# Late index products spread unevenly over the units of the first output projection, and four moves of single steps elsewhere

## The reference: two layers of a decoder trunk

```python
# layer 0
h = rms_norm(x, g);  z = h @ w_in                    # q, k, v, index q/k/w, u, v_b
logits = einsum('bqhe,bse->bqhs', qi, ki)            # 8 index heads of width 32
score  = einsum('bqh,bqhs->bqs', wi, relu(logits))   # causal
idx    = top_k(score, 256)                           # the keys that a query attends to
x = x + concat(a_out, b_out) @ w_out                 # sparse attention, spatial gating
x = x + square(relu(rms_norm(x) @ w1)) @ w2          # MLP, hidden 4096
# layer 1
y = conv31(glu(rms_norm(x) @ w_pw1)) + b;  x = x + silu(rms_norm(y, g_conv)) @ w_pw2
x = x + square(relu(rms_norm(x) @ w1)) @ w2
```

## Time and profile before

| | us |
|---|---|
| median of 3 runs | 2062.2 |
| the profiled execution | 2062.01 |
| its span, first to last instruction | 2060.3 |
| PE busy | 2028.5 |
| DVE busy | 1554.9 |
| ACT busy | 1040.8 |
| POOL busy | 863.9 |

### The profile page before, as it was taken

How to read it: one execution, slowest core, us unless ns; L and a number is a source line. 1 busy time by engine, 2 the same in 40 slices (tenths; PEclk the granted TensorE clock), 3 DMA queues, 4 the chain that set the end, 5 groups by cost and what they waited for, 6 DMA issues and landing times.

```text
span 2060.3 us, 28332 instructions
## 1 busy us (share of the span) xinstructions
PE 2028.5 (98%) x9594; PEld 1696.0 (82%) x9594; DVE 1554.9 (75%) x2238; ACT 1040.8 (51%) x1575; POOL 863.9 (42%) x572
## 2 busy tenths in 40 slices
PE   7999899999999999999999999999999999999999
PEld 7788788888889878888888888888878888888887
DVE  6698758988854377977888745889863577979877
ACT  6644666756446547453323256445365346463562
POOL 5864674654560110045646456858664700000000
PEclk9999999999999999999999999999999999999999
DMA  5221022423221245323232232323352463434433
GB/s 215 93 72 62 32 83 84 142 93 101 73 72 44 73 137 202 131 75 110 92 103 93 92 102 93 102 93 134 128 187 85 161 215 113 163 133 143 154 123 123
DMA packets 83043, 233.11 MB, mean 113 GB/s; under 512 B 7648, under 2 KB 8032, under 8 KB 81376
## 3 DMA queue, kind: packets, MB, share of 16 engines
q1 hardware_dynamic: 79312, 225.09, 32.5%
q10 hardware_dynamic: 3600, 6.32, 0.8%
HBM read 214.60 MB, written 16.78 MB: 112 GB/s over the span
## 4 chain that ended last, share of the span: by engine, by line
PE 83%; DVE 7%; issue 3%; POOL 3%; ACT 2%; DMA 1%; DVEq 0%; ACTq 0%; POOLq 0%; SPq 0%
PE psum L1077 16%; PE psum L1079 16%; PE psum L1078 16%; PE psum L1407 9%; PE psum L1408 9%; PE psum L1409 9%; PE psum L1252 3%; PE psum L1102 2%; DVE small L2614 2%; DVE score L2612 2%; PE psum L1228 1%; POOL w_buf L1464 1%; PE psum L1229 1%; DMA raw<-weights 1%; DVE psum L2862 1%
## 5 line engine op out<-in xcount | busy, mean ns | idle before, releaser
L1464 POOL TENSOR_TENSOR w_buf<-raw,w_buf 128x1024 fp32r<-128x1024 f32 x218 | 531.8, 2441 | 529.5 <-ACT w_buf L1834 508.4
L1834 ACT ACTIVATE w_buf<-raw 128x1024 fp32r<-128x1024 f32 x204 | 214.8, 1054 | 204.0 <-PE psum L1079 137.8
L1407 PE MATMUL psum<-hid_buf,w_buf 128*128 128x512 f32 x776 | 302.0, 389 | 1.4 <-issue 1.4
L1408 PE MATMUL psum<-hid_buf,w_buf 128*128 128x512 f32 x776 | 301.9, 389 | 0.0
L1409 PE MATMUL psum<-hid_buf,w_buf 128*128 128x512 f32 x776 | 301.9, 389 | 0.0
L1077 PE MATMUL psum<-hid_buf,w_buf 128*128 128x512 f32 x768 | 300.0, 391 | 1.0 <-POOL hid_buf L1632 1.0
L1078 PE MATMUL psum<-hid_buf,w_buf 128*128 128x512 f32 x768 | 299.1, 389 | 0.0
L1079 PE MATMUL psum<-hid_buf,w_buf 128*128 128x512 f32 x768 | 299.0, 389 | 0.0
L1078 PE MATMUL psum<-h_buf,w_buf 128*128 128x512 f32 x768 | 298.8, 389 | 0.0
L1079 PE MATMUL psum<-h_buf,w_buf 128*128 128x512 f32 x768 | 298.8, 389 | 0.0
L1077 PE MATMUL psum<-h_buf,w_buf 128*128 128x512 f32 x768 | 298.8, 389 | 0.0
(11 more groups left out here) (379 smaller groups left out, 3648.5 us busy)
## 6 DMA issues: line engine op xcount, KB each, us to landing
raw<-weights SPq DMA_DIRECT2D x298, 512.0 KB, 3.5
w_more<-weights SPq DMA_DIRECT2D x66, 512.0 KB, 4.1
xt<-x_t SPq DMA_DIRECT2D x2, 2048.0 KB, 8.8
x_early<-xt SPq DMA_DIRECT2D x2, 2048.0 KB, 10.2
h_first<-x_early SPq DMA_DIRECT2D x2, 2048.0 KB, 8.5
out_t<-xt SPq DMA_DIRECT2D x16, 256.0 KB, 2.0
x_in<-x_t SPq DMA_DIRECT2D x12, 256.0 KB, 6.4
m_kept<-m_ring ACTq DMA_DIRECT2D x12, 256.0 KB, 2.0
```

Source lines behind the costliest of these rows:

```text
L1407: nc.tensor.matmul(acc, hi, b_split(v, 0, j), start=start, stop=False, skip_group_check=True)
L1408: nc.tensor.matmul(acc, hi, b_split(v, 1, j), start=False, stop=False, skip_group_check=True)
L1464: nc.gpsimd.tensor_tensor(dst_lo, src, dst_hi.bitcast(F32), ALU.subtract).then_inc(done, 1)
L1834: nc.scalar.activation(w_buf[:, 0, :, slot * P:(slot + 1) * P], raw[:, slot % 2], ACT.Copy).then_inc(hi_up, 1)
```

## The change: counts for the products, room for the groups, and three reordered lists

- `late_logits`: units 0 to 7 get 2, 2, 2, 5, 5, 5, 5, 6 products instead of 4 each. `logits_behind` places them within a unit: behind steps 1 and 3 of a half unit; behind steps 0, 2, 3, 5, 7 with five; 0, 1, 3, 4, 5, 7 with six.
- `late_groups_at`: the unit before the last unit up of each 16 (u = 6, 22, 38) counts half. By the formula unit 7 has one group instead of two, 8 two instead of one, 17 two instead of one, 18 one instead of two, 21 two instead of one, 22 none instead of two, 23 two instead of one, 31 three instead of two, 38 one instead of two.
- `pre`: the mean stands before step 6 of block (1, 1, 0), six matmuls earlier.
- `split_first`: the weights of pair 0 are split behind unit 5, the first half of activations 1 behind unit 6; before, the other way round.
- `pair_splits`: in session 0 the copies of products 4 and 5 stand in step 4, behind the two splits of activations 2; before, in steps 5 and 6.

```diff
-    at = [sum(cost[:n + 1]) * len(free) / sum(cost) for n in range(len(cost))]
-    return [tiles for tiles, when in zip(LATE_GROUPS, at) if free.index(u) < when <= free.index(u) + 1
-            or (u == free[-1] and when > len(free))]
+    room = [0.5 if at % 16 == 6 else 1.0 for at in free]
+    before = sum(room[:free.index(u)])
+    at = [sum(cost[:n + 1]) * sum(room) / sum(cost) for n in range(len(cost))]
+    return [tiles for tiles, when in zip(LATE_GROUPS, at) if before < when <= before + room[free.index(u)]
+            or (u == free[-1] and when > sum(room))]
...
+LATE_COUNTS = (2, 2, 2, 5, 5, 5, 5, 6)
+
 def late_logits(m):
-    return range(LOGITS[LATE] + 4 * m, LOGITS[LATE] + 4 * m + 4)
+    first = LOGITS[LATE] + sum(LATE_COUNTS[:m])
+    return range(first, first + LATE_COUNTS[m])
+
+def logits_behind(logits, k, steps):
+    return [n for at, n in enumerate(logits) if (at + 1) * steps // len(logits) - 1 == k]
...
-                    if k % 2 and logits:
-                        index_logits(logits[k // 2])
+                    for n in logits_behind(logits, k, KT):
+                        index_logits(n)
...
-                    if logits:
-                        index_logits(logits[k])
+                    for n in logits_behind(logits, k, 4):
+                        index_logits(n)
...
                             for k in range(4 * kh, 4 * kh + 4):
+                                if (i, kh, r, k) == (1, 1, 0, 6):
+                                    mean_of("conv1", sum_lo)
...
-                            if (i, kh, r) == (1, 1, 0):
-                                mean_of("conv1", sum_lo)
...
                 if i and r == 1:
+                    split_weights(0)
+                if i and r == 2:
                     split_activations(1, 0)
-                if i and r == 2:
-                    split_weights(0)
...
-                    if g > first and copied(g - 1):
+                    if g > first and copied(g - 1) and not (session == 0 and g in (5, 6)):
                         copy_product(g - 1)
...
                     if session == 0 and g == 4:
                         split_activations(2, 0)
                         split_activations(2, 1)
+                        copy_product(4)
+                        copy_product(5)
```

## The result

The changed kernel takes 2065.9 us, the median of 22 runs (2064.0 to 2069.5); the kernel before took 2062.2 on the same chip (22 runs, 2061.5 to 2064.5). The ratio is 1.0016 [1.001, 1.0022]: slower by 3.7 us, which is within the 0.2% that counts as no change, but on the other side of it than the forecast (2061.2), and outside its range (2059.1 to 2063.0). The profiled execution took 2065.06 us with a span of 2063.3, 3.0 more than before.

The account below looks back on a forecast made before the run. PE was taken as the bound, busy 2028.5 of 2060.3 us, so only its stalls could change. The terms -0.65 - 0.1 - 1.4 + 1.2 = -0.95 took 2062.0 to 2061.1, median 2061.2 us, range 2059.1 to 2063.0.

Parts of the forecast that it names:

- the hidden tiles: Hidden tile 7 at 469.47 and 557.04: the first stall of 1.04 goes, the second grows by 0.95; net -0.1.
- the session: Session 0: stalls of 0.72 ahead of it and 1.68 at product 8 go, 0.97 returns at product 10; net -1.4.
- the mean of ff0 0: Stall at 340.10, behind the late products of wout 0: grows by 0.4, to 0.9 idle.
- Product 10: In session 0: waits for the copy of product 6, 0.7 idle, so 0.85 + 0.1 come back.
- the second hidden tile: Hidden tile 7 at 557.04: POOL's weights for unit 42 delay tile 39, stall grows by 0.95 to about 1.2 idle.
- the last rival: All four moves work as aimed, the mean of conv1 costs nothing: -6.3, 2055.9 us; chance 0.03.
- Late products: Part on wout 0: product stalls fall from 2.36 to 1.3, gain 1.05; mean of ff0 0 +0.4; net -0.65.
- the hand schedule: Units 0 to 3 of wout 0 worked forward by durations, engines in list order: two late products in unit 3, 0.3 and 0.8.
- The mean of conv1: At 1503.28: PE asks 1.36 us earlier, the sums come no earlier, 2.4 idle; +1.2, bounds 0 and +2.7.
- the wait at 1520: A PE wait of 0.2 behind the mean of conv1, which the shift of 1.2 to 1.4 may swallow.
- The spread only moves its waits: Rival on wout 0: unit 3 stalls for all that units 1 and 2 did, gain of 1.05 gone, 2062.2; chance 0.15.
- The other side: Rival: conv1's early mean delays weights three or four blocks on, 1.2 becomes 2.7, sum +0.5, 2062.7; chance 0.12.

Follow-up runs that it names:

- the first: The changed kernel with four late products in each unit as before, the other moves kept: 2063.2 us, ratio 1.0004.
- the seventh experiment: The changed kernel without the new product counts and without the early mean of conv1, leaving the top-k groups and session 0 moves: 2060.7 us, ratio 0.9989.
- the fourth: The changed kernel with the squares of wout 0 written by ACT to PSUM, so their sum has one SBUF input: 2061.2 us, ratio 0.9995.
- the fifth: The changed kernel with squares in PSUM and the mean of conv1 back behind its block: 2059.9 us, ratio 0.9988.
- the second experiment: The kernel before with the new counts of late products alone: 2065.0 us, ratio 1.0016.
- the third experiment: The changed kernel with the sum of squares of row 1 moved behind the residual of row 2 on DVE: 2061.9 us, ratio 0.9995.

## Why the prediction was wrong

**The bound and the method were right.** The work of PE didn't change, and stall by stall the traces add up: -1.04 and +0.9 at the hidden tiles and -1.4 in the session, as forecast, and +0.2 at the mean of ff0 0 (0.4 forecast). Product 10 is 0.78 idle (0.7 forecast), the second hidden tile 1.15 (1.2), no stall stands ahead of the session or at product 8. The third product of unit 3, for which 0.3 + 0.1 were forecast, isn't late. One share was reckoned wrong: 4.1 us is half of the 8.4 of all touched stalls and two thirds only of the 6.3 of the last rival.

**The step that failed** is in "Late products": "DVE does for it a residual and a sum of squares (0.68 each)". By the hand schedule "the residual of row 2 on DVE (299.9), which stands behind the low input of row 1", and the sum of squares between them was put in at its price without POOL. POOL's next weights were in that schedule as well: the relu behind ACT's split of unit 6 ends there at 299.2, so the split at about 298.6, and POOL has the low part of unit 6 from then to 301.0. The sum of squares, behind the low input (298.1) and a sum (0.6), begins at about 298.7, inside it. I had the rule for exactly this in the same part, from the Trainium skill ("SBUF — State Buffer", section "SBUF: two separate sides"), and applied it to the low input alone. By that rule the sum of squares, which also has two inputs in SBUF, isn't done until POOL is: the trace agrees (2.68 us, 0.55 past POOL's end, and 0.67 from PSUM). The residual was short beside POOL at all times; it has one input in PSUM.

In the rows of before only the low input is long, but these rows end at 331.9. Behind them the same trace has another such hold, the split of the sums, which took 2.77 us (DVE and POOL of the kernel before):

```profile
337.28 2.77 DVE L2431 TENSOR_TENSOR sum_lo<-sq_sum,sum_hi 128x512 fp32r<-128x512 f32 x1
336.94 2.55 POOL L1464 TENSOR_TENSOR w_buf<-raw,w_buf 128x1024 fp32r<-128x1024 f32 x1 [7.27 <-ACT w_buf L1834]
```

It too has two inputs in SBUF, and the stall at 340.10 waits for it, in the changed kernel as before; the +0.4 there was worked out from DVE's list alone. In the ten traces, from 286 to 345 us, 78 low inputs, sums of squares and splits of sums begin more than 0.15 us ahead of the end of POOL's weights. Every one ends 0.54 to 0.56 behind that end. What hid the hold of the sum of squares: in the kernel before, each of the six up to 325 us begins after one of POOL's weights has ended and ends before the next begins (the second from 300.13 to 300.81, POOL at work until 299.13 and from 301.82), so 0.68 was their price without POOL. The new spread makes both engines earlier, but not by the same: less the 1.08 of the start-up, this sum comes at 298.9 instead of 300.1, and POOL's next weights at 298.7 instead of 301.8.

**The term mis-sized.** -1.05 was forecast and +2.62 measured. Of the 3.7 between them, 2.2 is the longer stall (3.01 instead of 0.8) and about 1.5 the clock. The prediction said that a stall costs its idle time + 0.27. That holds up to some size. In the ten traces (before, after and eight experiments) the clock fell behind both stalls of 3.01, behind one of five at the early mean of conv1 (2.07 to 2.33 idle) and behind two of ten at the one near 216 us (1.65 to 1.69); behind none of 0.2 to 1.44 did it fall. The bounds of this part, -2.4 and +0.6, left out a hold of the sum of squares; the upper one should have had the wait for one more of POOL's instructions.

**The mean of conv1.** At full clock it cost 0.7 (alone in the kernel before), 0.8 (between the first and the seventh experiment) and 1.2 (between the fourth and the fifth), against +1.2 forecast. In the trace of the changed kernel PE loses 1.08 there, and 0.3 come back by 1525 us: the wait at 1520, of which the prediction said that it may be swallowed, is gone. What the prediction lacked is the price in clock: among the four kernels of the experiments that have the early mean, 23 of 44 runs are below 1.000; among the three experiments without it (and without the stall of 3.01), 6 of 29, and of the kernel before 15 of 61. The four are uneven: 7, 6, 3 and 7 of 11. The changed kernel (13 of 22 at 0.998) fits this, against 3 of 11 at 0.998 in the second experiment, which has the stall of 3.01 without the early mean. The trace of the third experiment shows the place once; in the four other traces with the early mean the clock held there. So that the early mean costs clock is likely and not shown, as a run leaves one trace.

**The rivals.** None of them was this. "The spread only moves its waits" had the place and the direction, but as a zero and not as a loss. The other side was sought at conv1, where it isn't.

**Open.** The trace doesn't say what decides whether the clock falls after an idle time of about 2 us. Executions of one kernel differ in it.

## What to carry to other kernels

When a schedule by hand uses a hold of one engine by another, apply it to every instruction of that kind in the stretch, not only to the one that the old trace shows lengthened: moving work changes which of them meets the other engine. Two remedies worked here: put the instruction that others wait for ahead of the one that can be held, or let one of its inputs come from PSUM. And a stall of PE of 2 us or more can cost more than its length, also where it is only asked for earlier: a wait brought forward by 1.4 us cost 0.7 to 1.2 at once, and half of the executions with it lost about 2 us of clock somewhere, against a quarter of those without.

## What was not expected of the hardware

- The same sum of 128x512 fp32 on DVE took 0.68 us alone, 1.60 and 2.68 beside POOL's 2.4 us weights, and 0.67 beside them with one input in PSUM.
- Where the clock fell behind a stall (five times in the ten traces), PE first worked on at full rate for 1.2 to 1.4 us, then about eight matmuls started 0.43 us apart instead of 0.23, which cost 1.5 to 1.8 us.
- The mean clock of a whole execution, 1.000, 0.999 or 0.998, goes with these stretches: a step of 0.001 is worth about 2 us of 2062, half of what a comparison of two kernels is asked to tell.
